# Gate and up weights of a macaron encoder block: split tiles of their own, 224 bytes off the 2 KB raster

## The chip, the cores and the metric

The kernel runs as one program on one core of a Trainium2 chip. The metric is the device time of one execution in microseconds (us), the median of several runs. SBUF, the memory that the engines work from, has 128 partitions; an address here is a byte offset within each partition. TensorE (PE in the profile) multiplies a stationary operand, which is loaded ahead of it (PEld), by a moving operand that streams through, and adds the result up in PSUM. VectorE (DVE), ScalarE (ACT), GpSimd (POOL) and the DMA queues (SP issues most of them) work beside it.

## The reference

One encoder layer over 512 frames of width 1024 in float32: a SwiGLU feed-forward at half weight, a token mixer, a second SwiGLU feed-forward at half weight, each with an RMS norm before and after.

```
def swiglu(h, w_gate, w_up, w_down):
    return (jax.nn.silu(h @ w_gate) * (h @ w_up)) @ w_down      # 1024 -> 4096 -> 1024

h = rms_norm(x, g_ffn1_pre)
x = x + 0.5 * rms_norm(swiglu(h, w_ffn1_gate, w_ffn1_up, w_ffn1_down), g_ffn1_post)
h = rms_norm(x, g_mix_pre)
proj = h @ w_in                                                 # 1024 -> 5632
... stick-breaking attention (8 heads x 64), retention (4 heads x 128), sigmoid merge gates
x = x + rms_norm(merged @ w_out, g_mix_post)
h = rms_norm(x, g_ffn2_pre)
x = x + 0.5 * rms_norm(swiglu(h, w_ffn2_gate, w_ffn2_up, w_ffn2_down), g_ffn2_post)
```

Both feed-forwards compute h @ w_gate and h @ w_up with 4096 columns each. These two products are what the change is about.

## The kernel before

**Split products.** Every float32 operand of TensorE is split in two parts of a reduced float32 format, hi and lo: ScalarE writes hi (a copy that rounds), VectorE writes lo = whole - hi. A product of two operands is then three matmuls: hi by hi, hi by lo, lo by hi. So each block of weights, 4 KB in each partition (1024 values), needs a tile `w_hi` and a tile `w_lo`, both split out of `w_raw` (where the DMA lands) or out of `w_sum` (a sum of two raw blocks).

**Gate and up (both feed-forwards).** Gate and up are taken together as 2 x 2 blocks and multiplied by a scheme of seven products in place of eight (Strassen's, in Winograd's form): the tokens are halved (256 each), the contraction is halved (512 each), and gate and up columns of a pair are two column blocks of 128. The loop runs over 16 pairs (`NG`); the first pair is taken by eight plain products. In each later pair PE runs the seven products in the order `PE_ORDER`; `product_of` (L804) calls `blocks` (L781), which issues 24 matmuls, one after another: for each of two column blocks f and four contraction blocks k the stationary operand is 128 columns of `w_hi` or `w_lo` (512 bytes in each partition), and 256 token columns of `a1`, `a21`, `a22` or the sums `s1` to `s4` stream past (1024 bytes). Lines 792, 794 and 795 are hi by hi, hi by lo, lo by hi; 777, 779 and 780 are the same three for the very first half block. Each matmul comes with its own load of the stationary operand. `PLACE` gives each of the seven products its own pair of tiles.

**Down.** The second product of the feed-forward uses seven products too, but the other way round: the stationary operand is 128 tokens of `l_hi` or `l_lo`, and 512 columns of `w_hi` or `w_lo` stream past (`down_unit`, lines 893 to 895). Its weights use the first four of the tile pairs in turn (`SLOTS`); `l_hi` and `l_lo` lie over the last three.

**Mixer.** Projections take one of the first four tile pairs as stationary operand and stream 512 columns of `h_hi` or `h_lo` (`product`, lines 725 to 727), or the other way round (`row_product`, 732 to 734). Between them stand the attention's own matmuls. Some of these (lines 1056 to 1066) have as stationary operand `tri`, a small constant tile that lies behind the other constants at the end of the arena, and stream 128 to 512 columns of `sp_hi`, `sp_lo`, `cum_hi` or `cum_lo`.

**Where tiles lie.** All tiles are placed by hand in one arena by `place`, which gives an offset. The arena starts 128 bytes past a multiple of 2048. `x_tok`, `h_hi`, `h_lo`, `w_raw`, then `w_hi0`, `w_lo0` (with `w_sum0` at the same place as `w_lo0`), `w_hi1` and so on follow one another, and each is a multiple of 4 KB, so each starts on the arena's own raster of 2048 bytes; `act_at` and `region` are asserted to lie on it (`LINE`). `tri` lies off it: its two halves start 864 and 1376 bytes past a raster point. So of every address that PE reads in the gate and up stage, stationary or moving, the offset from the raster is a multiple of 512.

**Order.** Each engine has its own instruction list, written by hand, and waits on semaphores. In the gate and up stage a weight tile is written again one pair later, when `unit_done` says that PE has finished the product that read it (`return_wait`, L1288, on ACT; `free`, L1811, on DVE). At the last pair `chunk_hi` (L1418) begins to write `l_hi` over the tiles of products 1, 2 and 6, one chunk for each finished product.

Of the kernel before, what the change touches and what calls it, by code (L numbers as in the profile page):

```python
# [7 lines left out]
ALU = mybir.AluOpType  # L8
ACT = mybir.ActivationFunctionType
F32 = mybir.dt.float32  # L10
F32R = mybir.dt.float32r

P = 128
T = 512
# [7 lines left out]
PAIRS = SBH * SBD // P  # L22
RMS_EPS, GN_EPS = 1e-6, 1e-5
ARENA = 212832
UNIT = KD * P
SLOTS = 4
# [11 lines left out]
PRODUCTS = 7  # L38
# [12 lines left out]
LEFT = 3  # L51

PLACE = {7: 0, 5: 1, 4: 2, 3: 3, 1: 4, 2: 5, 6: 6}

RAW11, RAW21, RAW12, RAW22 = range(4)
# [41 lines left out]
CONST_COLS = 514  # L97
CONST_BYTES = 2080
LINE = 2048

def constants():
# [108 lines left out]
def build(nc, x, gains, w_gate1, w_up1, w_down1, w_in, w_proj_sb, w_proj_ret, w_out,  # L211
          w_gate2, w_up2, w_down2, const, decay_t, rope_t, x_mid, out):
    with ExitStack() as ctx:
# [3 lines left out]
        top = [0]  # L217

        def place(name, shape, dt=F32, at=None):
            size = -(-int(np.prod(shape[1:])) * 4 // 32) * 32  # L220
            off = top[0] if at is None else at
            if at is None:
                top[0] += size
            assert off + size <= ARENA, (name, off + size)
            return nc.alloc_sbuf_tensor_at(name, shape, dt, offset=base + off), off + size

        small_at = ARENA - 5 * 32 - 8 * P - CONST_BYTES
# [15 lines left out]
        h_lo, _ = place("h_lo", [P, KD, T], F32R)  # L244
        w_raw, _ = place("w_raw", [P, SLOTS, UNIT])

        w_hi, w_lo, w_sum = [], [], []
        for i in range(PRODUCTS):
            if i == SLOTS:

                mix_at = top[0]
            w_hi.append(place(f"w_hi{i}", [P, UNIT], F32R)[0])
            w_sum.append(place(f"w_sum{i}", [P, UNIT], at=top[0])[0])
            w_lo.append(place(f"w_lo{i}", [P, UNIT], F32R)[0])
        act_at = top[0]
        assert act_at % LINE == 0

# [53 lines left out]
        b22_hi, e = place("b22_hi", [P, UNIT], F32R, at=e)  # L313
        a21_hi, e = place("a21_hi", [P, KH, HALF], F32R, at=act_at + quarter + 4096)
        b22_lo, e = place("b22_lo", [P, UNIT], F32R, at=act_at + quarter + 12288)
# [6 lines left out]
        decay, e = place("decay", [P, RH, T], at=mix_at)  # L322
        rope, e = place("rope", [P, 2, T], at=e)
        region = e
        assert region % LINE == 0

        en = region + 6 * D * 4

# [16 lines left out]
        qk_r, e3 = place("qk_r", [P, 2, T], at=e3)  # L345
        g_r, e3 = place("g_r", [P, T], at=e3)
        proj_t, e3 = place("proj_t", [P, T], at=e3)
        oe = (small_at - 4 * PAIRS * T * 4) // LINE * LINE
        assert e3 <= oe, (e3, oe)
        o_sb_hi, e4 = place("o_sb_hi", [P, PAIRS, T], F32R, at=oe)  # L350
        o_sb_lo, e4 = place("o_sb_lo", [P, PAIRS, T], F32R, at=e4)
# [18 lines left out]
        w_hi_done, w_lo_done, unit_done = sem("w_hi_done"), sem("w_lo_done"), sem("unit_done")  # L370
# [142 lines left out]
        def bank_two(first):  # L513
# [5 lines left out]
        T_ORDER = (7, 6, 4, 5)  # L519
        N_SUMS = 3 * (NG - 1)  # L520

        FIRST_AT = {RAW11: (w_hi[PLACE[1]], w_lo[PLACE[1]]), RAW21: (w_hi[PLACE[2]], w_lo[PLACE[2]]),
                    RAW12: (w_hi[PLACE[6]], w_lo[PLACE[6]]), RAW22: (b22_hi, b22_lo)}

        block = ctx.enter_context(nc.Block())

# [175 lines left out]
        def _(pe):  # L702
# [99 lines left out]
            def product_of(m, bank):  # L802
                stream = {1: A11, 2: A12, 3: (s4_hi, s4_lo), 4: A22, 5: (s1_hi, s1_lo), 6: (s2_hi, s2_lo),
                          7: (s3_hi, s3_lo)}[m]  # L804
                blocks(bank, (w_hi[PLACE[m]], w_lo[PLACE[m]]), *stream, m in (1, 2, 7), m in (2, 3, 4)
                       ).then_inc(unit_done, 1)

            def first_gate(fi, u0, half, d):
# [199 lines left out]
            for ev in events:  # L1008
                if ev[0] == "mm":
                    f, k = ev[1], ev[2]  # L1010
# [166 lines left out]
        def _(act_eng):  # L1177
# [98 lines left out]
            def weights_hi(fi, u0, p, m):  # L1276

                slot = PLACE[m]
                if m in (1, 2, 3):
                    raw = {1: RAW11, 2: RAW21, 3: RAW22}[m]  # L1280
                    act_eng.wait_ge(raw_full[raw], p * 16 + (raw_turn(u0) * 16 + 16))
                    return_wait(u0, p, m)
                    act_eng.activation(w_hi[slot][:, :], w_raw[:, raw, :], ACT.Copy).then_inc(w_hi_done, 1)  # L1283
                else:
                    sum_made(fi, p, m)
                    act_eng.activation(w_hi[slot][:, :], w_sum[slot][:, :], ACT.Copy).then_inc(w_hi_done, 1)  # L1286

            def return_wait(u0, p, m):  # L1288

# [123 lines left out]
            def chunk_hi(fi, ud, n):  # L1413
                ph, c = divmod(n, CHUNKS)
                m = DOWN_ORDER[ph]

                act_eng.wait_ge(unit_done, ud + 2 * (n - LEFT) + 2 if n >= LEFT else ud - PRODUCTS + n + 1)
                if m == 1:  # L1418
                    act_eng.wait_ge(a_done, NF * fi + 2 * CHUNKS * (c + 1))
                elif m in (7, 6, 5, 3):  # L1420
                    act_eng.wait_ge(f_sum, 16 * fi + CHUNKS * (7, 6, 5, 3).index(m) + c + 1)
                act_eng.activation(l_hi[n % LEFT][:, :, :], left_of(m, c), ACT.Copy).then_inc(l_hi_done, 1)
# [251 lines left out]
        def _(dve):  # L1674
# [115 lines left out]
            def weights_lo(fi, u0, p, m):  # L1790
                slot = PLACE[m]
                dve.wait_ge(w_hi_done, p * PRODUCTS + (u0 + SPLIT_ORDER.index(m) + 1))
                if m in (1, 2, 3):
                    whole_w = w_raw[:, {1: RAW11, 2: RAW21, 3: RAW22}[m], :]
                else:
                    if m in (6, 7):

                        dve.wait_ge(t_done, p * 4 + (fi * N_T - {6: 1, 7: 2}[m]))
                    whole_w = w_sum[slot][:, :]
                dve.tensor_tensor(w_lo[slot][:, :], whole_w, w_hi[slot][:, :].bitcast(F32), ALU.subtract  # L1800
                                  ).then_inc(w_lo_done, 1)

            def first_lo(u0, i):
# [542 lines left out]
```

## Time and profile before

| | |
|---|---|
| device time, median of 3 runs | 1382.3 us (1382.27 to 1382.37) |
| span of the profiled execution, first to last instruction | 1380.3 us |
| outside the span | 2.0 us, the difference of the two (the profiled execution's own device time is not given beside its span) |
| PE busy / PEld busy | 1365.8 us (99%) / 1226.0 us (89%) |
| DVE busy / ACT busy | 1031.3 us (75%) / 734.2 us (53%) |
| DMA queue of SP | 34.6% of the 16 engines' span |

How to read it. "Busy" is the part of the span in which an engine has at least one instruction under way. PE's instructions overlap: one matmul is counted from its start until its last result is out, and the next has started long before that. The mean ns of one matmul is therefore not what it costs in a row of many; that is the distance from start to start, called the pitch below. The span goes from the first to the last instruction.

### The profile page before, as it was taken

The numbers are of one execution on the slowest core, as the hardware profiler recorded it, in microseconds if no ns is written. First come the engines' busy times: TensorE is split into PE (matmuls) and PEld (weight loads), VectorE is DVE, ScalarE is ACT, GpSimd is POOL, SyncE is SP. The second block draws the span as 40 slices with busy tenths as digits, with TensorE's granted clock in tenths as the row PEclk, the third lists the DMA queues.
The fourth block names the chain that finished last, engine by engine and source line by source line (L and its number), as shares of the span: only waits on it lengthen the run. The fifth ranks groups of instructions, "written<-read, shape, count | busy, mean of one in ns | idle before, by whom it ended". The sixth has DMA issues, their size and how long they took to land.

```text
span 1380.3 us, 22732 instructions
## 1 busy us (share of the span) xinstructions
PE 1365.8 (99%) x8668; PEld 1226.0 (89%) x8668; DVE 1031.3 (75%) x1124; ACT 734.2 (53%) x1008; POOL 99.9 (7%) x156
## 2 busy tenths in 40 slices
PE   8999999999999999999999999999999999999998
PEld 7999999999888888777778888899999999988886
DVE  7987887787988964767664344689778778888896
ACT  6544544545675652666663333555455445458563
POOL 0000000000340000222210000000000000025100
PEclk9999999999999999999999999999999999999999
DMA  6323332336995555212113345233233233399844
GB/s 206 108 83 115 122 96 86 122 108 237 193 206 156 175 206 132 68 58 64 47 46 92 92 132 188 92 122 116 85 122 108 79 117 122 100 283 197 178 142 153
DMA packets 152935, 177.71 MB, mean 129 GB/s; under 512 B 5552, under 2 KB 116400, under 8 KB 152752
## 3 DMA queue, kind: packets, MB, share of 16 engines
q1 hardware_dynamic: 139536, 151.54, 34.6%
q0 software_dynamic: 13056, 25.17, 10.1%
q8 instruction: 35, 0.57, 0.2%
q10 hardware_dynamic: 288, 0.26, 0.1%
q14 instruction: 20, 0.16, 0.0%
HBM read 170.66 MB, written 6.29 MB: 128 GB/s over the span
## 4 chain that ended last, share of the span: by engine, by line
PE 93%; DVE 3%; ACT 1%; DMA 1%; issue 1%; POOL 0%; SPq 0%; DVEq 0%; ACTq 0%; POOLq 0%
PE ps L792 15%; PE ps L795 15%; PE ps L794 15%; PE ps L893 7%; PE ps L894 7%; PE ps L895 7%; PE ps L725 6%; PE ps L727 5%; PE ps L726 5%; PE ps L732 2%; PE ps L734 2%; PE ps L733 2%; PE ps L1085 1%; DMA w_raw<-w_ffn_up 1%; PE ps L1040 1%; PE ps L1047 1%
## 5 line engine op out<-in xcount | busy, mean ns | idle before, releaser
L792 PE MATMUL ps<-s_hi,w_hi 128*128 128x256 f32 x960 | 271.9, 283 | 0.5 <-DVE w_lo L1800 0.5
L795 PE MATMUL ps<-s_hi,w_lo 128*128 128x256 f32 x960 | 271.7, 283 | 0.0
L794 PE MATMUL ps<-s_lo,w_hi 128*128 128x256 f32 x960 | 271.7, 283 | 0.0
L792 PE MATMUL ps<-a_hi,w_hi 128*128 128x256 f32 x808 | 229.0, 283 | 1.1 <-DVE a_lo L1755 1.1
L794 PE MATMUL ps<-a_lo,w_hi 128*128 128x256 f32 x808 | 228.7, 283 | 0.0
L795 PE MATMUL ps<-a_hi,w_lo 128*128 128x256 f32 x808 | 228.6, 283 | 0.0
L1286 ACT ACTIVATE w_hi<-w_sum 128x1024 fp32r<-128x1024 f32 x120 | 123.9, 1056 | 174.7 <-DVE w_sum L1829 80.1
L792 PEld LDWEIGHTS ps<-s_hi,w_hi 128*128 128x128 f32 x960 | 184.3, 192 | 0.8 <-DVE w_lo L1800 0.7
L794 PEld LDWEIGHTS ps<-s_lo,w_hi 128*128 128x128 f32 x960 | 184.3, 192 | 0.0
L795 PEld LDWEIGHTS ps<-s_hi,w_lo 128*128 128x128 f32 x960 | 184.3, 192 | 0.0
L893 PE MATMUL ps<-w_hi,l_hi 128*128 128x512 f32 x448 | 174.7, 390 | 0.0
L895 PE MATMUL ps<-w_hi,l_lo 128*128 128x512 f32 x448 | 174.4, 389 | 0.0
L894 PE MATMUL ps<-w_lo,l_hi 128*128 128x512 f32 x448 | 174.3, 389 | 0.0
L792 PEld LDWEIGHTS ps<-a_hi,w_hi 128*128 128x128 f32 x808 | 155.1, 192 | 1.5 <-issue 1.5
L794 PEld LDWEIGHTS ps<-a_lo,w_hi 128*128 128x128 f32 x808 | 155.1, 192 | 0.0
L795 PEld LDWEIGHTS ps<-a_hi,w_lo 128*128 128x128 f32 x808 | 155.1, 192 | 0.0
L1800 DVE TENSOR_TENSOR w_lo<-w_sum,w_hi 128x1024 fp32r<-128x1024 f32 x120 | 141.7, 1221 | 1.5 <-ACT w_hi L1286 1.1
L1678 DVE TENSOR_TENSOR w_lo<-w_raw,w_hi 128x1024 fp32r<-128x1024 f32 (+1 forms) x66 | 72.0, 1095 | 93.7 <-ACT w_hi L1186 93.3
L1800 DVE TENSOR_TENSOR w_lo<-w_raw,w_hi 128x1024 fp32r<-128x1024 f32 x90 | 109.9, 1223 | 37.0 <-ACT w_hi L1283 36.9
L2284 POOL DMA_DIRECT2D d_sum<-w_ffn_down x48 | 58.7, 1470 | 914.3 <-DVE w_raw L2001 860.3
L725 PE MATMUL ps<-h_hi,w_hi 128*128 128x512 f32 x288 | 118.6, 412 | 0.4 <-DVE w_lo L1678 0.4
L727 PE MATMUL ps<-h_hi,w_lo 128*128 128x512 f32 x288 | 112.5, 390 | 0.0
(222 smaller groups left out, 2529.1 us busy)
## 6 DMA issues: line engine op xcount, KB each, us to landing
w_raw<-w_ffn_gate SPq DMA_DIRECT2D x64, 512.0 KB, 5.0
w_raw<-w_ffn_up SPq DMA_DIRECT2D x64, 512.0 KB, 4.6
d_sum<-w_ffn_down POOLq DMA_DIRECT2D x48, 512.0 KB, 12.2
w_raw<-w_in SPq DMA_DIRECT2D x44, 512.0 KB, 3.9
w_raw<-w_ffn_down SPq DMA_DIRECT2D x40, 512.0 KB, 4.4
d_sum<-w_ffn_down SPq DMA_DIRECT2D x16, 512.0 KB, 7.9
x_tok<-x SPq DMA_DIRECT2D x8, 512.0 KB, 6.0
d_m_raw<-w_ffn_down SPq DMA_DIRECT2D x8, 512.0 KB, 8.3
```

The costliest lines, as they stand in the source:

```text
L725: pe.matmul(ps[:, bank, out_cols], wh, src_hi, start=first, stop=False)
L726: pe.matmul(ps[:, bank, out_cols], wh, src_lo, start=False, stop=False)
L727: return pe.matmul(ps[:, bank, out_cols], wl, src_hi, start=False, stop=last)
L792: pe.matmul(o, wh, hi[:, k, :], start=first and f == 0 and k == 0, stop=False, skip_group_check=True)
L794: pe.matmul(o, wh, lo[:, k, :], start=False, stop=False, skip_group_check=True)
L795: mm = pe.matmul(o, wl, hi[:, k, :], start=False, stop=last and k == KH - 1, skip_group_check=True)
L893: pe.matmul(o, sh, wh[:, cols], start=first and g == 0, stop=False, skip_group_check=True)
L894: pe.matmul(o, sh, wl[:, cols], start=False, stop=False, skip_group_check=True)
L895: mm = pe.matmul(o, sl, wh[:, cols], start=False, stop=last and g == 1, skip_group_check=True)
L1286: act_eng.activation(w_hi[slot][:, :], w_sum[slot][:, :], ACT.Copy).then_inc(w_hi_done, 1)
L1678: dve.tensor_tensor(w_lo[slot][:, 0:cols], w_raw[:, slot, 0:cols], w_hi[slot][:, 0:cols].bitcast(F32), ALU.subtract).then_inc(w_lo_done, 1)
L1800: dve.tensor_tensor(w_lo[slot][:, :], whole_w, w_hi[slot][:, :].bitcast(F32), ALU.subtract).then_inc(w_lo_done, 1)
```

## The change

The tiles that the gate and up stage uses are new ones, `u_hi`, `u_lo` and `w_sum` of each product. They lie where `w_hi` and `w_lo` lie, but 224 bytes higher (`UP_OFF`), so that each starts 224 bytes past a raster point. The stages that use `w_hi` and `w_lo` keep the names. Since the seventh `u_lo` now ends 224 bytes further up, and the fourth one too, everything from the fifth tile pair upward (`w_hi4` to `w_hi6`, `mix_at`, `act_at` and all that is placed from them: `l_hi`, `act`, `a21`, `b22`, `s3`, the mixer's tiles) moves up by 512 bytes (`GAP`); two asserts and one rounding that asked for 2048 now ask for 512. `b22`, the weights of one of the eight blocks of the first pair, is not among the `u` tiles: it moves by 512, not by 224. One wait changes: since a chunk of `l_hi` and `l_lo` now lies over the tiles of two products, `chunk_hi` waits for one product more (at most the third). No instruction is added, taken away or moved on any engine; only addresses differ, and that one count.

```diff
@@ build: the tiles @@
-        w_hi, w_lo, w_sum = [], [], []
+        w_hi, w_lo, u_hi, u_lo, w_sum = [], [], [], [], []
+        raster = top[0]
+        mix_at = raster + 2 * SLOTS * UNIT * 4 + GAP
         for i in range(PRODUCTS):
-            if i == SLOTS:
-
-                mix_at = top[0]
-            w_hi.append(place(f"w_hi{i}", [P, UNIT], F32R)[0])
-            w_sum.append(place(f"w_sum{i}", [P, UNIT], at=top[0])[0])
-            w_lo.append(place(f"w_lo{i}", [P, UNIT], F32R)[0])
-        act_at = top[0]
-        assert act_at % LINE == 0
+            at = raster + 2 * i * UNIT * 4 + (GAP if i >= SLOTS else 0)
+            w_hi.append(place(f"w_hi{i}", [P, UNIT], F32R, at=at)[0])
+            w_lo.append(place(f"w_lo{i}", [P, UNIT], F32R, at=at + UNIT * 4)[0])
+            at = raster + 2 * i * UNIT * 4
+            u_hi.append(place(f"u_hi{i}", [P, UNIT], F32R, at=at + UP_OFF)[0])
+            at += UNIT * 4
+            w_sum.append(place(f"w_sum{i}", [P, UNIT], at=at + UP_OFF)[0])
+            u_lo.append(place(f"u_lo{i}", [P, UNIT], F32R, at=at + UP_OFF)[0])
+        act_at = raster + 2 * PRODUCTS * UNIT * 4 + GAP
...
-        assert region % LINE == 0
+        assert region % GAP == 0
...
-        oe = (small_at - 4 * PAIRS * T * 4) // LINE * LINE
+        oe = (small_at - 4 * PAIRS * T * 4) // GAP * GAP
@@ the tiles that the first pair, the seven products and their splits use @@
-        FIRST_AT = {RAW11: (w_hi[PLACE[1]], w_lo[PLACE[1]]), RAW21: (w_hi[PLACE[2]], w_lo[PLACE[2]]),
-                    RAW12: (w_hi[PLACE[6]], w_lo[PLACE[6]]), RAW22: (b22_hi, b22_lo)}
+        FIRST_AT = {RAW11: (u_hi[PLACE[1]], u_lo[PLACE[1]]), RAW21: (u_hi[PLACE[2]], u_lo[PLACE[2]]),
+                    RAW12: (u_hi[PLACE[6]], u_lo[PLACE[6]]), RAW22: (b22_hi, b22_lo)}
...
-                blocks(bank, (w_hi[PLACE[m]], w_lo[PLACE[m]]), *stream, m in (1, 2, 7), m in (2, 3, 4)
+                blocks(bank, (u_hi[PLACE[m]], u_lo[PLACE[m]]), *stream, m in (1, 2, 7), m in (2, 3, 4)
...
-                    act_eng.activation(w_hi[slot][:, :], w_sum[slot][:, :], ACT.Copy).then_inc(w_hi_done, 1)
+                    act_eng.activation(u_hi[slot][:, :], w_sum[slot][:, :], ACT.Copy).then_inc(w_hi_done, 1)
...
-                act_eng.wait_ge(unit_done, ud + 2 * (n - LEFT) + 2 if n >= LEFT else ud - PRODUCTS + n + 1)
+                act_eng.wait_ge(unit_done, ud + 2 * (n - LEFT) + 2 if n >= LEFT else ud - PRODUCTS + min(n + 2, LEFT))
...
-                dve.tensor_tensor(w_lo[slot][:, :], whole_w, w_hi[slot][:, :].bitcast(F32), ALU.subtract
+                dve.tensor_tensor(u_lo[slot][:, :], whole_w, u_hi[slot][:, :].bitcast(F32), ALU.subtract
```

## Rows read from the trace of the kernel before

**Rows 1.** The page: busy time of two engines; the chain that ended last, by engine.
```profile
PE 1365.8 (99%) x8668; PEld 1226.0 (89%) x8668; DVE 1031.3 (75%) x1124; ACT 734.2 (53%) x1008; POOL 99.9 (7%) x156
PE 93%; DVE 3%; ACT 1%; DMA 1%; issue 1%; POOL 0%; SPq 0%; DVEq 0%; ACTq 0%; POOLq 0%
```

**Rows 2.** Groups of PE: line, output<-inputs, columns, xcount | busy us, mean ns
```profile
L792 PE MATMUL ps<-s_hi,w_hi 128*128 128x256 f32 x960 | 271.9, 283 | 0.5 <-DVE w_lo L1800 0.5
L792 PE MATMUL ps<-a_hi,w_hi 128*128 128x256 f32 x808 | 229.0, 283 | 1.1 <-DVE a_lo L1755 1.1
L792 PE MATMUL ps<-a_hi,b_hi 128*128 128x256 f32 x32 | 9.1, 286 | 0.0
L777 PE MATMUL ps<-a_hi,w_hi 128*128 128x256 f32 x8 | 2.4, 296 | 0.6 <-DVE a_lo L1740 0.6
L893 PE MATMUL ps<-w_hi,l_hi 128*128 128x512 f32 x448 | 174.7, 390 | 0.0
```

**Rows 3.** Windows inside both gate and up stages: busy us (xinstructions), PEclk, DMA.
```profile
core 0: us, PE busy (x) PEld busy (x) DVE busy (x) ACT busy (x) POOL busy (x), PEclk, DMA share, GB/s
100.00:200.00 100.00, 100.00 (x836) 100.00 (x835) 79.14 (x80) 49.56 (x60) 0.00 (x0) 1.00 0.34 105
950.00:1050.00 100.00, 100.00 (x836) 100.00 (x835) 80.47 (x81) 49.74 (x61) 0.00 (x0) 1.00 0.35 106
```

**Rows 4.** Timeline of PE in the gate and up stage: start us, duration us.
```profile
200.04 0.28 PE L792 MATMUL ps<-s_hi,w_hi 128*128 128x256 f32 x1
...
203.88 0.28 PE L795 MATMUL ps<-a_hi,w_lo 128*128 128x256 f32 x1
```

**Rows 5.** Timeline of PE in a mixer projection of 512 columns, settled.
```profile
569.05 0.39 PE L725 MATMUL ps<-h_hi,w_hi 128*128 128x512 f32 x1
569.28 0.39 PE L726 MATMUL ps<-h_lo,w_hi 128*128 128x512 f32 x1
569.50 0.39 PE L727 MATMUL ps<-h_hi,w_lo 128*128 128x512 f32 x1
569.73 0.39 PE L725 MATMUL ps<-h_hi,w_hi 128*128 128x512 f32 x1
```

**Rows 6.** Groups of PE in the window 572.44:573.70, stationary operand `tri`.
```profile
L1066 PE MATMUL ps<-cum_lo,tri 128*128 128x256 f32 x2 | 0.6, 280 | 0.0
L1064 PE MATMUL ps<-cum_hi,tri 128*128 128x256 f32 x2 | 0.6, 279 | 0.0
```

**Rows 7.** Groups of PE in the window 581.45:583.10, `tri` with 512 columns.
```profile
L1059 PE MATMUL ps<-sp_lo,tri 128*128 128x512 f32 x2 | 0.8, 397 | 0.0
L1056 PE MATMUL ps<-sp_hi,tri 128*128 128x512 f32 x2 | 0.8, 396 | 0.0
```

**Rows 8.** Groups of PE in 21.97:22.80, just after a gap, tiles on the raster.
```profile
L794 PE MATMUL ps<-a_lo,w_hi 128*128 128x256 f32 x3 | 0.8, 281 | 0.0
L795 PE MATMUL ps<-a_hi,w_lo 128*128 128x256 f32 x2 | 0.6, 280 | 0.0
```

**Rows 9.** Groups of PE in 567.10:568.30, just after a gap, 512 columns, on the raster.
```profile
L726 PE MATMUL ps<-h_lo,w_hi 128*128 128x512 f32 x2 | 0.8, 395 | 0.0
```

**Rows 10.** Timeline of the weight loads (PEld): two that follow the transposes.
```profile
21.75 0.19 PEld L792 LDWEIGHTS ps<-a_hi,w_hi 128*128 128x128 f32 x1
21.86 0.19 PEld L794 LDWEIGHTS ps<-a_lo,w_hi 128*128 128x128 f32 x1
```

**Rows 11.** Timeline of ACT at the end of the first gate and up stage.
```profile
330.20 0.60 ACT L1326 ACTIVATE u_c<-ps 128x512 f32<-128x512 f32 x1 [1.45 <-PE ps L795]
330.70 1.05 ACT L1422 ACTIVATE l_hi<-act 128x1024 fp32r<-128x1024 f32 x1
333.08 0.60 ACT L1334 ACTIVATE m_c<-ps 128x512 f32<-128x512 f32 x1 [1.33 <-PE ps L795]
333.58 1.05 ACT L1442 ACTIVATE w_hi<-w_raw 128x1024 fp32r<-128x1024 f32 x1
334.53 1.05 ACT L1422 ACTIVATE l_hi<-act 128x1024 fp32r<-128x1024 f32 x1
```

More of the change, by code:

```diff
@@ L99 @@
 LINE = 2048
+GAP = 512
+UP_OFF = 224
 def constants():
@@ L1282, in weights_hi @@
                     return_wait(u0, p, m)
-                    act_eng.activation(w_hi[slot][:, :], w_raw[:, raw, :], ACT.Copy).then_inc(w_hi_done, 1)
+                    act_eng.activation(u_hi[slot][:, :], w_raw[:, raw, :], ACT.Copy).then_inc(w_hi_done, 1)
                 else:
                     sum_made(fi, p, m)
-                    act_eng.activation(w_hi[slot][:, :], w_sum[slot][:, :], ACT.Copy).then_inc(w_hi_done, 1)
+                    act_eng.activation(u_hi[slot][:, :], w_sum[slot][:, :], ACT.Copy).then_inc(w_hi_done, 1)
             def return_wait(u0, p, m):
```

## The prediction

> **What bounds the kernel now.** I read the page first. PE is busy for 99% of the span, and 93% of the chain that ended last is PE [rows 1]. The table of groups shows why that share says little about single instructions: the matmuls of one form have a mean of 283 ns [rows 2], and the 5304 of them (counted below) end to end would be 1501 us, more than the span. So the next view is one that shows the pace. The windows in the middle of both gate and up stages have 836 matmuls in 100 us and PE without a gap [rows 3]. The timeline gives the pitch, from start to start: from 200.04 to 203.88 us there are 32 steps, so 120.0 ns each [rows 4]. In the 512-column products three steps take 0.68 us, 227 ns each [rows 5]. In both places the granted clock is at its upper level of 2.4 GHz (PEclk 1.00) [rows 3].
>
> From these two pitches: 256 more columns cost 107 ns, 0.418 ns a column, which is one cycle of 2.4 GHz. What is left is 120 - 107 = 13 ns per matmul, the same at 256 and at 512 columns. That fixed part is where a change of addresses could act. Nothing else in this stage can give time: PE never waits there, and DVE, next to it, is busy for 79% and 80% of it [rows 3].
>
> How many matmuls are concerned: three lines with 960 and 808 each, 3 x 1768 = 5304; three lines with 32 on `b_hi` and `b_lo`, 96; three with 8, 24 [rows 2]. Together 5424, at 120 ns 651 us, 47% of the span. The 96 on `b22` keep an offset that is a multiple of 512, so 5424 - 96 = 5328 get the new one.
>
> **The change part by part.** Nothing is issued more or less often, so every term is a change of duration.
>
> *The 224 bytes, seen by PE.* In the stage as it is, every pair of addresses that PE reads at one time is apart by a multiple of 512, and the pitch is 120 for all of them. The trace has one tile off the raster that PE reads as stationary operand, `tri`. With 256 columns its matmuls last 279 and 280 ns against 283 [rows 6, 2]. Duration and pitch go together: 283 with 120, 390 with 227 [rows 2, 4, 5], so the pitch is the duration less 163. For `tri` that makes 116 to 117 ns. I take 117, a saving of 3 ns, since the rows of `tri` are the nearest there are: same number of columns, same format, stationary operand off the raster. They aren't the same case. `tri` is 352 bytes past a multiple of 512 and the new tiles 224, and its matmuls come at most four in a row with others between. 5328 x 3.0 ns = 16.0 us.
>
> The bounds of this term. Below: two loads of such weights stand 110 ns apart at 21.75 and 21.86 us [rows 10], where the load did not have to share its time with a settled stream; each matmul needs one load, so I take 110 as the floor. 10 ns x 5328 = 53 us saved. Above: the same `tri` with 512 columns lasts 396 to 397 ns against 390, 7 ns more [rows 2, 7]. If 256 columns paid that, it would be 7 x 5328 = 37 us lost. Between ends this far apart I stay with the row of equal width.
>
> *A doubt, from the raster itself.* Durations of 280 and 281 ns also occur with all tiles on the raster, right behind a gap, before the stream goes back to 283 [rows 8]; at 512 columns the same phase costs more, 395 against 390 [rows 2, 9]. So the cost of a load beside a stream depends on how the two meet, and after a gap they meet otherwise than settled. This bears the term out in sign, shorter at 256 columns and longer at 512 when not in step, but says too that the short rows of `tri` may be an unsettled phase and not an effect of its address.
>
> Here the Trainium skill speaks against the change. In "TensorE: Matmul & The Clock Gate", section "Step-by-step: what each phase is for", it says that TensorE has two independent read ports, one for the moving operand and one for the weights, and that loading the next weights takes no read bandwidth from the running matmul. By that rule no address could matter and the sum would be 0; the 7 ns of [rows 7] do not fit it well. The same page's section "Back-to-back issue gap" gives N/2.4 + 2.5 ns, an estimate of 109 ns here, by which the sum would be -58 us if all of the excess were a collision; the trace's 120 is 11 ns above it.
>
> *The 512 bytes.* `l_hi`, `s3`, `a21`, `b22`, `act`, the mixer's tiles and `w_hi4` to `w_hi6` move by 512. PE reads today at offsets of 0, 512, 1024 and 1536 past the raster (the column blocks of a weight tile), with one pitch for all; the means and the 836 in 100 us leave no room for one slow quarter [rows 2, 3]. I cost it at 0.
>
> *ACT and DVE on the new tiles.* Their seven splits and four sums a pair now start 224 bytes off. No row shows such an operation alone. A pair takes 7 x 24 x 0.12 = 20.16 us, of which DVE is idle for a fifth, about 4.1 us [rows 3]; with 11 operations on these tiles each could grow by 0.37 us before PE waits. At 117 ns a pair lasts 19.66 us and the cover is 3.6 us; at the floor of 110 it is 18.5 us and 2.5 us. So 0, between no change and that cover; DVE would become the bound only below some 95 ns. ACT has half of its time free.
>
> *The later wait of `chunk_hi`.* Chunk 0 now waits for the second product of the last pair, chunk 1 for the third. On ACT chunk 0 stands behind the copy `u_c`, which itself waits for the third product and starts at 330.20; chunk 1 stands behind `m_c` and a split that start at 333.08 and 333.58 [rows 11]. Both waits are met before they are reached: 0. Without that cover chunk 0 would be a product later, 24 x 0.12 = 2.9 us, with the down splits of ACT and then of DVE queued behind it, and PE's first down unit behind those.
>
> **Sum.** -16.0 us on the span of 1380.3, 1364.3; the median of the runs is 2.0 us above the span, so 1366.3 us, 1.2% less.
>
> **The rivals.**
>
> *A, the forecast:* 116 to 118 ns settled, 1366 (1361 to 1372). For it: [rows 6]. Against it: [rows 8].
>
> *B, no effect:* the 13 ns are a fixed price of changing weights, and the stream settles at 120 wherever the tile lies. For it: the excess is the same at 256 and 512 columns, and four column blocks at four offsets make no difference; the rows of `tri` are short. Against it: `tri` is shorter in each group at 256 and longer at 512, as after a gap. Time: 1382.
>
> *C, much of the 13 ns is a collision that an offset takes away:* the pitch goes to between 110 and 114, near the floor of the load. For it: the spacing in [rows 10], and that an excess of 13 ns is there at all. Against it: nothing at 256 columns in the trace is settled below 116. At 112 ns: 8 x 5328 = 43 us, 1340 (1329 to 1350).
>
> *D, slower:* off the raster a load that is spread over two 512-byte pieces collides for longer, as in [rows 7]. Place: every matmul of `blocks`. Price: 7 ns, 37 us, 1420; it decides from a settled pitch of 120.5 on, since 0.5 ns x 5328 is 2.8 us. Against it: the same tile gains at 256 columns.
>
> The skill's rule on two ports is B's mechanism; that no address tells in the settled stream agrees with it [rows 3], the rows of `tri` don't [rows 6, 7].
>
> **How the numbers follow.** A 0.42, B 0.22, C 0.20, D 0.16. The forecast is A's 1366.3. What this kernel's measurement tells from no change is 0.2%, 2.8 us. Faster is A and C, 0.62; same is B, 0.22; slower is D, 0.16. The range reaches from C's floor, 1329, over A and B to 1386, which takes in a small loss; what is left out is nearly all of D.
>
> **What the profile after would show.** A: the mean of L792, L794 and L795 on `u_hi` and `u_lo` is 280 where it was 283, a window of 100 us in the stage has 857 matmuls in place of 836, and 32 steps take 3.74 us. The group on `b_hi` stays at 283 when settled, L893 at 390, and the mixer as it is. PE goes on without a gap in the windows. C: means of 273 to 277, and over 877 in the window. B: 283 and 836. D: 287 or more. The 512 bytes are wrong at zero if L893 or L725 move by 1 ns or more. The cover of DVE is wrong if PE in the windows shows idle time released by `u_lo`. The wait of `chunk_hi` is wrong if the first `l_hi` comes later after `u_c` than now, or if PE waits at the start of down. The forecast as a whole is wrong if the settled pitch is outside 116 to 118.

## The result, and the profile after

The changed kernel takes 1366.32 us, the median of four runs (1366.27, 1366.30, 1366.35 and 1368.69). The kernel before takes 1382.28 us in the same session. The ratio is 0.9889, 95% interval 0.9875 to 0.9903: 1.1% faster, 16.0 us. In the sessions of the later runs the kernel before took 1382.14 to 1382.32 us, so that all times below can be laid side by side. The profiled execution has a span of 1364.3 us against 1380.3.

The page of the changed kernel: busy time of the engines, the chain that ended last by engine, then groups (line, engine, operation, output<-inputs, shape, count | busy us, mean ns | idle before and who ended it). The lines are five further down than in the kernel before: L792, L794, L795 are now L797, L799, L800.

```profile
PE 1349.2 (99%) x8668; PEld 1209.1 (89%) x8668; DVE 1029.3 (75%) x1124; ACT 734.3 (54%) x1008; POOL 99.9 (7%) x156
PE 91%; DVE 4%; ACT 2%; DMA 1%; issue 1%; POOL 0%; SPq 0%; DVEq 0%; ACTq 0%; POOLq 0%
L797 PE MATMUL ps<-s_hi,u_hi 128*128 128x256 f32 x960 | 268.0, 279 | 1.5 <-DVE u_lo L1805 0.8
L797 PE MATMUL ps<-a_hi,u_hi 128*128 128x256 f32 x808 | 225.7, 279 | 1.1 <-DVE a_lo L1760 1.1
L1291 ACT ACTIVATE u_hi<-w_sum 128x1024 fp32r<-128x1024 f32 x120 | 124.0, 1057 | 173.0 <-DVE w_sum L1834 80.3
L797 PEld LDWEIGHTS ps<-s_hi,u_hi 128*128 128x128 f32 x960 | 180.5, 188 | 2.1 <-ACT m_c L1325 1.1
L898 PE MATMUL ps<-w_hi,l_hi 128*128 128x512 f32 x448 | 174.9, 390 | 0.1
```

Against [rows 2] the matmuls of the split weights went from 283 to 279 ns, and their idle time from 0.5 to 1.5 us. The products of `down` (L898) stayed at 390 ns. PE is still busy for 99%, but its share of the chain that ended last fell from 93% to 91%, and that of DVE rose from 3% to 4% [rows 1]. Both small moves mean something, as will be seen.

Windows in the middle of both gate and up stages, to be laid beside [rows 3], with the columns given there:

```profile
100.00:200.00 100.00, 100.00 (x860) 100.00 (x859) 81.68 (x83) 51.63 (x64) 0.00 (x0) 1.00 0.35 108
950.00:1050.00 100.00, 100.00 (x859) 100.00 (x859) 81.67 (x83) 49.64 (x60) 0.00 (x0) 1.00 0.34 105
```

And two rows of the timeline of PE, 32 steps apart, as in [rows 4] (start us, duration us):

```profile
200.06 0.28 PE L800 MATMUL ps<-a_hi,u_lo 128*128 128x256 f32 x1
...
203.79 0.28 PE L799 MATMUL ps<-s_lo,u_hi 128*128 128x256 f32 x1
```

24 matmuls more in 100 us, and 3.73 us for 32 steps where it was 3.84. With the starts in nanoseconds the mean pitch is 116.67, that is 280 cycles of 2.4 GHz in place of 288. At 512 columns it is 226.7 ns, 544 cycles, in both kernels. So I shall write the pitch as columns plus a number of cycles: N + 32 on the raster for both widths, and N + 24 for the new tiles.

From the first to the last matmul of a gate and up stage the time fell from 328.33 to 319.56 us in the first feed-forward and from 328.07 to 320.39 in the second, 16.46 us together (first start to last start). All the rest of the program got longer by 0.47 us. So the gain is where it was looked for.

### The profile page after: what moved, and what is told of

Same layout as the page of the kernel before. It is cut to its first block, busy times and chain, and to the rows that moved or that the text cites. A ratio compares the mean times of both kernels' runs of the same rounds, so it can differ in the third digit from the quotient of the medians.

```text
span 1364.3 us, 22732 instructions
## 1 busy us (share of the span) xinstructions
PE 1349.2 (99%) x8668; PEld 1209.1 (89%) x8668; DVE 1029.3 (75%) x1124; ACT 734.3 (54%) x1008; POOL 99.9 (7%) x156
## 4 chain that ended last, share of the span: by engine, by line
PE 91%; DVE 4%; ACT 2%; DMA 1%; issue 1%; POOL 0%; SPq 0%; DVEq 0%; ACTq 0%; POOLq 0%
PE ps L797 14%; PE ps L800 14%; PE ps L799 14%; PE ps L898 8%; PE ps L899 7%; PE ps L900 7%; PE ps L730 6%; PE ps L732 5%; PE ps L731 5%; PE ps L737 2%; PE ps L738 2%; PE ps L739 2%; PE ps L1090 1%; DMA w_raw<-w_ffn_up 1%; PE ps L1045 1%
## 5 line engine op out<-in xcount | busy, mean ns | idle before, releaser
L797 PE MATMUL ps<-s_hi,u_hi 128*128 128x256 f32 x960 | 268.0, 279 | 1.5 <-DVE u_lo L1805 0.8
L800 PE MATMUL ps<-s_hi,u_lo 128*128 128x256 f32 x960 | 267.7, 279 | 0.0
L799 PE MATMUL ps<-s_lo,u_hi 128*128 128x256 f32 x960 | 267.7, 279 | 0.0
L797 PE MATMUL ps<-a_hi,u_hi 128*128 128x256 f32 x808 | 225.7, 279 | 1.1 <-DVE a_lo L1760 1.1
L800 PE MATMUL ps<-a_hi,u_lo 128*128 128x256 f32 x808 | 225.4, 279 | 0.0
L799 PE MATMUL ps<-a_lo,u_hi 128*128 128x256 f32 x808 | 225.3, 279 | 0.0
L1291 ACT ACTIVATE u_hi<-w_sum 128x1024 fp32r<-128x1024 f32 x120 | 124.0, 1057 | 173.0 <-DVE w_sum L1834 80.3
L797 PEld LDWEIGHTS ps<-s_hi,u_hi 128*128 128x128 f32 x960 | 180.5, 188 | 2.1 <-ACT m_c L1325 1.1
L799 PEld LDWEIGHTS ps<-s_lo,u_hi 128*128 128x128 f32 x960 | 180.5, 188 | 0.0
L800 PEld LDWEIGHTS ps<-s_hi,u_lo 128*128 128x128 f32 x960 | 180.5, 188 | 0.0
L898 PE MATMUL ps<-w_hi,l_hi 128*128 128x512 f32 x448 | 174.9, 390 | 0.1
L797 PEld LDWEIGHTS ps<-a_hi,u_hi 128*128 128x128 f32 x808 | 151.9, 188 | 1.6 <-issue 1.5
L799 PEld LDWEIGHTS ps<-a_lo,u_hi 128*128 128x128 f32 x808 | 151.9, 188 | 0.0
L800 PEld LDWEIGHTS ps<-a_hi,u_lo 128*128 128x128 f32 x808 | 151.9, 188 | 0.0
L1805 DVE TENSOR_TENSOR u_lo<-w_sum,u_hi 128x1024 fp32r<-128x1024 f32 x120 | 141.6, 1219 | 1.5 <-ACT u_hi L1291 1.1
```

The lines of the kernel that those rows point to most:

```text
L797: pe.matmul(o, wh, hi[:, k, :], start=first and f == 0 and k == 0, stop=False, skip_group_check=True)
L799: pe.matmul(o, wh, lo[:, k, :], start=False, stop=False, skip_group_check=True)
L800: mm = pe.matmul(o, wl, hi[:, k, :], start=False, stop=last and k == KH - 1, skip_group_check=True)
L898: pe.matmul(o, sh, wh[:, cols], start=first and g == 0, stop=False, skip_group_check=True)
L1291: act_eng.activation(u_hi[slot][:, :], w_sum[slot][:, :], ACT.Copy).then_inc(w_hi_done, 1)
L1805: dve.tensor_tensor(u_lo[slot][:, :], whole_w, u_hi[slot][:, :].bitcast(F32), ALU.subtract).then_inc(w_lo_done, 1)
```

## The experiments

Two things had to be told apart first: the change has two edits (224 bytes for the split tiles, 512 bytes for the others, with the wait of `chunk_hi`), and my theory was that only the first acts. Then came what the 224 bytes do. "Distance" below is the address of the stationary operand less that of the streamed one, modulo 512.

**gap_only: the 512 bytes and the wait alone.**

```
-UP_OFF = 224
+UP_OFF = 0
```

> All addresses of the change but the 224: the gate and up weights stand on the raster again (offset 0), everything from the fifth tile pair up stays 512 bytes higher, and the later wait of chunk_hi stays. Theory (the gain is the 224 bytes as PE's weight loads see them): settled pitch 120 ns (duration 283), 836 matmuls in 100 us, and 1382.3 us within 0.1%. Rival (part of the gain, or a hidden loss, comes from the 512 bytes or the wait): another time, 1366 to 1381 if the 512 bytes help, over 1384 if they cost.

Measured: 1382.27 us, the median of 11 runs (1382.05 to 1382.53), ratio to the kernel before 1.0000, interval 0.9991 to 1.0009. The windows of it:

```profile
100.00:200.00 100.00, 100.00 (x836) 100.00 (x835) 79.12 (x80) 49.55 (x60) 0.00 (x0) 1.00 0.34 105
950.00:1050.00 100.00, 100.00 (x836) 100.00 (x835) 80.18 (x81) 49.73 (x61) 0.00 (x0) 1.00 0.35 107
```

836 as before, and the time too. The whole gain belongs to the 224 bytes.

**all_off: the weights of the mixer and of `down` 224 bytes off as well.**

```
-w_hi.append(place(..., at=at)[0])
-w_lo.append(place(..., at=at + UNIT * 4)[0])
+w_hi.append(place(..., at=at + UP_OFF)[0])
+w_lo.append(place(..., at=at + UNIT * 4 + UP_OFF)[0])
```

> The tiles of the down stage and of the mixer get the 224 bytes too, so all weights of all stages stand off the raster. There, matmuls of 512 columns run: 1344 in down and 384 in the mixer with the weights as the moving operand, 1056 with the weights as the stationary one, settled at 227 ns. Theory (as the short rows of tri at 512 columns showed, 396 to 397 ns against 390): +7 ns each where the load or the stream is off the raster, 2784 x 7 = 19 us, so about 1386 us. Rival (a settled stream gains at 512 columns as it did at 256, 3.3 ns each): 2784 x 3.3 = 9 us less than the changed kernel, 1357 us. Second rival (only the stationary operand's address counts, and the moving one's does not): down as in the changed kernel, the mixer's 1056 alone move.

Measured: 1380.89 us, ratio to the kernel before 0.9993 (0.9984 to 1.0002). One of its 11 runs was at 1386.06, the others between 1380.71 and 1381.03. Gate and up kept their new pace, and the 512-column matmuls lost what it had brought. Timeline of PE in the mixer of this kernel, to be laid beside [rows 5]:

```profile
749.69 0.40 PE L730 MATMUL ps<-h_hi,w_hi 128*128 128x512 f32 x1
749.92 0.39 PE L731 MATMUL ps<-h_lo,w_hi 128*128 128x512 f32 x1
750.15 0.40 PE L732 MATMUL ps<-h_hi,w_lo 128*128 128x512 f32 x1
750.39 0.39 PE L730 MATMUL ps<-h_hi,w_hi 128*128 128x512 f32 x1
```

A window and one group of the same kernel:

```profile
100.00:200.00 100.00, 100.00 (x860) 100.00 (x859) 81.64 (x83) 51.59 (x64) 0.00 (x0) 1.00 0.35 108
```

```profile
L898 PE MATMUL ps<-w_hi,l_hi 128*128 128x512 f32 x448 | 177.4, 396 | 0.0
```

Three steps take 0.70 us where they took 0.68: the mean is 233.3 ns, N + 48. `down` moved by the same amount, 390 to 396 ns, although there the weights are the streamed operand and `l_hi` the stationary one. Added up over the 2746 steps of this width from one product with weights to the next, the stream takes 647.3 us where it took 631.9 in the changed kernel, so 15.4 more, and the kernel is 14.6 us longer. The expectation had 19 us, from 7 ns each; one reason may be that those of the mixer with stationary weights have a mean of 227.8 ns in the changed kernel, not 226.7, so they had less to lose. The price that [rows 7] shows for `tri` was real and holds in a settled stream; it belongs to 512 columns.

**scan_low and scan_high: other offsets, one for each of the seven tile places.**

```
-UP_OFF = 224
+UP_OFFS = (0, 32, 64, 96, 128, 160, 192)          # scan_low
+UP_OFFS = (224, 256, 288, 320, 352, 384, 448)     # scan_high
... at=at + UP_OFFS[i]
```

> The seven products have their weights at seven offsets: product 7 at 0, 5 at 32, 4 at 64, 3 at 96, 1 at 128, 2 at 160, 6 at 192 bytes past the raster. One profile then shows seven pitches. Theory 1 (fine grain: what counts is whether the offset is an odd multiple of 32 bytes, as 224 and the 352 of tri are): 117 ns at 32, 96 and 160, 120 at 0, 64, 128 and 192. Theory 2 (a load that lies over a 512-byte boundary is the cheap one): 120 at 0 alone, 117 at all others. Theory 3 (the offset in time between the load's reads and the stream's counts): graded, from 120 at 0 falling towards 117 near 224. The whole between 1366 and 1382 us.

> The same with product 7 at 224, 5 at 256, 4 at 288, 3 at 320, 1 at 352, 2 at 384, 6 at 448 bytes. Theory 1 (odd multiples of 32): 117 at 224, 288 and 352, 120 at 256, 320, 384 and 448. Theory 2 (512-byte boundary): 117 at all seven. Theory 3 (graded): 117 or less around 224 to 288, rising to 120 towards 448. The whole between 1366 and 1382 us, or under 1366 if an offset is better than 224.

One run each: 1374.47 and 1372.87 us. The mean pitch by offset, over both stages:

```
offset      0     32     64     96    128    160    192
ns      119.5  118.3  117.7  117.4  118.4  120.0  117.7
offset    224    256    288    320    352    384    448
ns      117.8  120.1  118.1  114.3  119.7  118.5  117.9   first feed-forward
        117.7  119.8  118.3  117.7  117.5  118.3  117.6   second feed-forward
```

None of the three theories stands. Odd multiples of 32 are not a class of their own (160 costs as much as 0), and a load that lies over a 512-byte boundary is not the cheap one (160 again, and 256). But 256 costs what 0 costs, 288 what 32 costs. And 320 gave two different means in one run. In the first feed-forward, 320 settled within three matmuls of each group; ten steps of it in scan_high:

```profile
96.01 0.28 PE L799 MATMUL ps<-s_lo,u_hi 128*128 128x256 f32 x1
...
97.14 0.28 PE L800 MATMUL ps<-s_hi,u_lo 128*128 128x256 f32 x1
```

That is 113 ns, a pitch that my forecast had only for its case C. Groups of 24 with neighbours of other offsets are a mixed state, so the next runs held one offset through a whole stage.

**shift_all_b: the kernel before, with all its tiles but the constants 96 bytes further on.**

```
-offset=base + off
+offset=base + off + (SHIFT if off < small_at else 0)      # SHIFT = 96
```

> The kernel before with all its tiles but the small constants group at the end moved together by 96 bytes: weights and streams keep their distance in multiples of 512, only their absolute address changes. Theory (the distance between the addresses that PE reads at one time counts): 120 ns and 227 ns as before, 1382.3 us. Rival (the absolute address of the weights counts, as if a load that does not start on its boundary were the cheap one): a pitch under 119 in the gate and up stage, 1364 to 1377 us; and at 512 columns 233 in place of 227, as in the kernel with all weights off the raster.

Measured: 1382.20 us, the median of 10 runs (1381.99 to 1382.57), ratio to the kernel before 1.0001 (0.9991 to 1.0011); 835 and 836 matmuls in the two windows. So an address off the raster does nothing by itself. What acts is where the tiles lie to each other.

**Three kernels with two offsets, one in each feed-forward.** Each stage has a set of split tiles of its own; the rest is as in the change.

```
-UP_OFF = 224
+UP_OFFS = (320, 96)     # or (64, 192), or (288, 448), indexed by the feed-forward
```

> The first feed-forward has its gate and up weights 320 bytes off the raster, the second 96 bytes, each for the whole stage, so that the stream can settle. In the kernels with seven offsets in one stage it did not (116.7 at 224 when alone, 117.8 among others), so their means don't tell which is best. Theory (each distance has its own settled pitch, and the order of the mixed means holds): 320 settles under 116.7, at 113 to 116, and 96 near 117. Rival (off the raster one settled price for all, 24 cycles a load): 116.7 in both stages.

> 64 bytes in the first feed-forward, 192 in the second. Theory (each distance its own price, mixed means 117.8 and 117.6): 116 to 119, not equal. Rival (one price off the raster): 116.7 in both. A third reading, that multiples of 64 count as on the raster, would give 120 in both; the mixed means speak against it.

> 288 bytes in the first feed-forward, 448 in the second. 288 and 224 lie equally far from 256, 448 and 64 equally far from the raster. Theory (each distance its own price, in a circle of 512 bytes but not symmetric, since a load reads ahead of a stream): 288 differs from the 116.7 of 224, 448 from what 64 gives. Rival (one price off the raster): 116.7 in both.

One run each: 1360.13, 1361.09 and 1372.53 us. Windows of the three kernels, in this order:

```profile
100.00:200.00 100.00, 100.00 (x885) 100.00 (x884) 84.45 (x85) 52.06 (x65) 0.00 (x0) 1.00 0.39 120
950.00:1050.00 100.00, 100.00 (x855) 100.00 (x854) 80.48 (x82) 50.95 (x62) 0.00 (x0) 1.00 0.35 107
```

```profile
100.00:200.00 100.00, 100.00 (x885) 100.00 (x884) 84.45 (x85) 52.05 (x65) 0.00 (x0) 1.00 0.39 120
950.00:1050.00 100.00, 100.00 (x852) 100.00 (x851) 80.38 (x81) 50.66 (x62) 0.00 (x0) 1.00 0.35 107
```

```profile
100.00:200.00 100.00, 100.00 (x848) 100.00 (x847) 80.24 (x82) 50.24 (x61) 0.00 (x0) 1.00 0.34 105
950.00:1050.00 100.00, 100.00 (x852) 100.00 (x851) 80.31 (x81) 49.95 (x61) 0.00 (x0) 1.00 0.34 105
```

The settled pitches are 113.3 ns for 320 and for 64 (N + 16), 117.3 for 96, 117.8 for 192 and for 448, 118.3 for 288. So each distance has a price of its own, and the rival (116.7 for all) is out. Offsets that differ by 256 agree (0 and 256, 32 and 288, 64 and 320, 192 and 448), so I read the price as one of the distance modulo 256. One thing in the second feed-forward doesn't fit one price for each distance: at 192 and at 448 the last products of the first pair and the first two of the next ran at 113.3 ns, and behind the wait ahead of product 6 the pitch was 117.8 for the rest of the stage. In [rows 6] `tri` lies at 352, which is 96 modulo 256, and 96 settles with durations of 280 ns: the short rows of `tri` were the effect of its address, and my doubt about an unsettled phase was not needed for them.

**u64: one offset of 64 for all seven places.**

```
-UP_OFF = 224
+UP_OFF = 64
```

> The changed kernel with 64 in place of 224, in both feed-forwards. Theory (the price of a load beside a settled stream depends on the distance between load and stream modulo 256 bytes: 32 cycles of 2.4 GHz at 0, 24 at 224, 16 at 64): pitch 113.3 ns, 880 matmuls or a few more in 100 us, and 5328 x 3.3 = 17.8 us under the changed kernel, less 1 us that PE waits more in the first pairs: 1349 to 1351 us. Rival (113.3 is near what DVE or the loads allow, and the second feed-forward does not reach it): 1352 to 1360 us, with PE waiting for u_lo in the windows.

Measured: 1360.98 us, ratio to the kernel before 0.9819 (0.9793 to 0.9844). The theory had 1349 to 1351, and the six runs lie on three levels: 1351.1 and 1351.3; 1360.9, 1361.0 and 1361.2; 1371.2. Five are faster than the change, one is slower. The profiled run was the slowest, and its windows are:

```profile
100.00:200.00 100.00, 100.00 (x851) 100.00 (x850) 80.74 (x83) 50.66 (x62) 0.00 (x0) 1.00 0.34 105
950.00:1050.00 100.00, 100.00 (x852) 100.00 (x851) 80.31 (x82) 50.20 (x61) 0.00 (x0) 1.00 0.34 105
```

Its pitch is 117.8 ns in both stages, where the same offset had 113.3 in two_64_192_b. So one offset has two paces, and each can hold through a stage. The first gate and up stage took 322.5 us here and 312.5 in two_64_192_b, 10.0 us apart, which is the distance between two levels. So I read the levels as none, one or both feed-forwards at the fast pace; the fast levels themselves were not profiled in this kernel.

**all_64: the other weights at 64 too** (the edit of all_off, with 64).

> The same 64 bytes for the weights of the down stage and the mixer too. In the mixer's 1056 matmuls with the weights as the stationary operand the distance is then 64, in the 1728 where the weights stream it is -64, that is 192 modulo 256. Theory (the same distance is cheap at 512 columns as at 256, as 224 is not: 16 cycles where the load is the later address): under 227 ns in the mixer's projections, 220 to 226; at 192 dearer than 227. Rival (at 512 columns the raster is the best there is, since the load needs only half of the stream's time and any other distance costs more): 228 to 234 in both.

One run: 1358.53 us. Windows and two groups:

```profile
100.00:200.00 100.00, 100.00 (x885) 100.00 (x884) 84.46 (x85) 52.16 (x65) 0.00 (x0) 1.00 0.38 120
950.00:1050.00 100.00, 100.00 (x885) 100.00 (x884) 84.46 (x86) 52.92 (x64) 0.00 (x0) 1.00 0.37 114
```

```profile
L898 PE MATMUL ps<-w_hi,l_hi 128*128 128x512 f32 x448 | 174.4, 389 | 0.0
L899 PE MATMUL ps<-w_lo,l_hi 128*128 128x512 f32 x448 | 175.7, 392 | 0.0
```

Both stages at the fast pace here. The 512-column matmuls pay 233.2 ns in the mixer, where the distance is 64, and a mean of 229.0 in `down`, where it is -64, that is 192 modulo 256. On the raster they pay 226.7. So the rival's 228 to 234 holds, and the theory's 220 to 226 doesn't. Less what this costs (the mixer and the two `down` stages are 8.1 us longer than in u64), the kernel would have taken 1350.5 us, near the fastest level of u64.

**l64: u64 with the activations of `down` (`l_hi`, `l_lo`) moved to 64 modulo 256,** to ask if a distance of +64 would help at 512 columns, in the stage where -64 cost little.

> u64, and in the down stage l_hi and l_lo, the stationary operand there, stand 64 bytes off the raster (at 320, which is 64 modulo 256), while the streaming weights stay on it: 1344 matmuls of 512 columns at distance 64. Theory: the distance of 64 costs 16 cycles at 512 columns too, 220 ns, 1344 x 6.7 = 9 us under u64. Rival (the raster is the best at 512 columns): 228 to 234 ns, 2 to 9 us over u64.

Measured: 1373.91 us (two runs near 1368.7, two near 1379.1), ratio to the kernel before 0.9927 (0.9901 to 0.9954). `down` settled at 233.3 ns and its group at

```profile
L899 PE MATMUL ps<-w_hi,l_hi 128*128 128x512 f32 x448 | 177.3, 396 | 0.0
```

So no: of the distances tried (0, 32, 64, 192, 224), the raster is the best for 512 columns. The two levels, 10.4 us apart, are the upper two of u64 again, some 8 us higher, which is about what 1340 matmuls cost at 6.6 ns more (8.8 us).

**reset64: can the fast pace be forced?** In the profiles with one offset to a stage the pace changed only at two kinds of place: where PE had waited, and where it passed a group on the raster (the product with `b22`, which no variant takes off the raster).

```
-UP_OFF = 224
+UP_OFFS = (64, 256, 288, 320, 320, 320, 320)
```

> Only the offsets of the gate and up tiles differ from the change: 64 for product 7, 256 for 5, 288 for 4, and 320 (64 modulo 256) for 3, 1, 2 and 6. Product 5 is in effect on the raster again, and is passed once in every pair. Theory (the phase in which a group of matmuls begins decides which of the two regimes an offset of 64 modulo 256 gets; the group on the raster wipes the phase that came before, and from 288 to 320 the stream falls to 113.3 ns, as product 3 did in each pair of the scan from 224 to 448): five products at 113.3 ns, product 5 at 120 and product 4 at 118.2, mean 115.0 ns, 5.0 ns less than the kernel before, 5328 x 5.0 = 26.6 us, some 1356 us, with all runs within 0.2% of each other. Rival 1 (the draw takes place at the gaps of PE alone, and passing an offset changes nothing): levels some 10 us apart between runs, as with one offset of 64 for all, and a regime that stays the same through a stage. Rival 2 (behind 0 and 32 the stream goes to the slow regime of 117.5, as product 4 did in the scan from 0 to 192): 7 products at a mean of 118 ns, some 1372 us, all runs alike.

One sentence in that expectation is wrong: product 3 reached 113.3 in the settled pairs of the first feed-forward of scan_high only, not in the second (118). Measured: 1372.79 us, the median of 5 runs (1372.07 to 1373.10), ratio to the kernel before 0.9931 (0.9917 to 0.9944). That is rival 2, 1372 with all runs alike, and my theory fell. The profile shows how. Timeline of PE at the end of product 7 (offset 64), in product 5 (offset 256), and further on at offset 320:

```profile
941.52 0.28 PE L797 MATMUL ps<-s_hi,u_hi 128*128 128x256 f32 x1
...
945.26 0.28 PE L797 MATMUL ps<-s_hi,u_hi 128*128 128x256 f32 x1
...
945.62 0.28 PE L797 MATMUL ps<-s_hi,u_hi 128*128 128x256 f32 x1
...
948.02 0.28 PE L800 MATMUL ps<-s_hi,u_lo 128*128 128x256 f32 x1
...
955.10 0.28 PE L800 MATMUL ps<-a_hi,u_lo 128*128 128x256 f32 x1
...
959.81 0.28 PE L797 MATMUL ps<-s_hi,u_hi 128*128 128x256 f32 x1
```

33 steps of 113.3 ns, behind a wait. Then 20 steps of 120.0 on what is in effect the raster. Then 40 steps of 117.8 at an offset that had 113.3 in two_320_96_b, and this pace at that offset for the rest of the stage. The levels are gone because the fast pace has no chance to last.

Does a group on the raster always lead to the slow pace? The traces say no, and show what goes with it. Behind the groups with `b22` in the first pair of a stage, 64 and 320 came out at 117.8 ns in 15 of 16 passes of the kernels that held them for a whole stage. The sixteenth is in the second feed-forward of all_64 (two starts behind the first group with `b_hi`, 69 steps apart, then two behind the second, 40 apart):

```profile
897.07 0.28 PE L797 MATMUL ps<-a_hi,u_hi 128*128 128x256 f32 x1
...
904.89 0.28 PE L797 MATMUL ps<-a_hi,u_hi 128*128 128x256 f32 x1
...
908.35 0.28 PE L800 MATMUL ps<-a_hi,u_lo 128*128 128x256 f32 x1
...
913.06 0.28 PE L797 MATMUL ps<-a_hi,u_hi 128*128 128x256 f32 x1
```

113.3 ns first, 117.8 then. Both groups have a mean of 120.0 ns when the first steps are left out. But in nanoseconds the second one goes 120, 120, 120, and the first one 118, 117, 121, 120, 124, over and over. scan_high has the same pair of patterns at its offset of 256: the same five unequal steps (within 1 ns) in all 15 pairs of the first feed-forward, where 320, two products further on, falls to 113.3, and 120s, even within 1 ns or so, in all 15 of the second, where 320 stays at 117.8. In reset64 the steps are even in all 30 passes, and only once did 320 run at 113.3 behind them, with a short wait of PE in between (at 930.63 us). So the raster doesn't wipe the history: the stream has two rhythms there as well, with one mean, and in these traces the even one led to the slow pace at 64 and 320, the uneven one to the fast. At 192 and 448 the pitch behind even 120s was 113.3, in four of four passes. So 117.8 may be one of two settled paces of 192 and 448 too; no run held the fast one for a stage.

## Why the prediction was right

The forecast was 1366.3 us, of case A, and the measurement 1366.32. The mechanism was right: the 224 bytes shorten the pitch, and the other edits cost nothing. That the two numbers agree to 0.1 us is luck: two terms were off, against each other, and the main one was read from a tile at another distance.

*The count and the pace.* The 5328 matmuls are right. The term of 3.0 ns was taken from durations in whole nanoseconds and is 3.33 in the trace (120.0 to 116.67), so the term is 17.8 us and not 16.0. The mean of the group is 279 where I said 280, the window has 860 where I said 857, and 32 steps take 3.73 us where I said 3.74. The `b_hi` group keeps 283 ns as its median, as its distance, still a multiple of 512, asks. The prediction cites [rows 3] for the clock in the mixer too, which those windows don't cover; a window of 568 to 570 us shows PEclk 1.00 there as well.

*The row that the term was read from.* The rows of `tri` did show an effect of address, but not that of 224 bytes: its distance counts as 96, and 96 has a pace of 117.3 when settled. That 224 has nearly the same, 116.7, nobody could read from `tri`. Had `tri` lain at 64, the same reading would have given 113 or 118.

*The 512 bytes and the wait of `chunk_hi`.* Both together at zero in gap_only, 1382.27 against 1382.28 us. In the changed kernel's timeline of ACT the first `l_hi` still starts 0.50 us behind the start of `u_c`, as in [rows 11]:

```profile
321.82 0.60 ACT L1331 ACTIVATE u_c<-ps 128x512 f32<-128x512 f32 x1 [1.23 <-PE ps L800]
322.32 1.05 ACT L1427 ACTIVATE l_hi<-act 128x1024 fp32r<-128x1024 f32 x1
```

*The cover of ACT and DVE.* The splits cost the same off the raster (ACT 1057 ns where it was 1056, DVE 1219 where it was 1221), so the address term is zero. But "a faster PE meets no wait" was read off the settled windows, and pairs 1 and 2 of the second feed-forward are not settled. PE's rows with a wait there, in the changed kernel:

```profile
915.88 0.38 PE L797 MATMUL ps<-s_hi,u_hi 128*128 128x256 f32 x1 [0.85 <-DVE u_lo L1805]
...
936.40 0.39 PE L797 MATMUL ps<-s_hi,u_hi 128*128 128x256 f32 x1 [0.65 <-ACT m_c L1325]
```

Before, the first of these was 0.45 us (the 0.5 in [rows 2]), and in place of the second was a start only 0.14 us late, without idle time. The chain of waits, followed back from there in the changed kernel (start us, length us), shows whose pace it is; the first eight rows lead to the first wait, the others, later, to the second:

```profile
904.41 0.68 DVE act L1884
905.09 2.27 DVE s_lo L1792 x2
907.36 0.82 DVE u_lo L1805
908.42 1.22 DVE u_lo L1805
909.63 1.15 DVE w_sum L1829
910.80 1.24 DVE w_sum L1841
912.22 1.05 issue
913.27 1.23 DVE w_sum L1848
...
923.35 3.87 DMA w_raw<-w_ffn_up
...
934.83 1.04 ACT u_hi L1291
935.87 0.49 ACT m_c L1325
```

The chain has no piece of PE between 899.84 and 936.40 us. Ahead of the first wait DVE has the streamed sums and the weights to do at once. From its `act` to PE's start this takes 11.47 us (904.41 to 915.88), and it took 11.47 before (913.01 to 924.48): PE only comes earlier to the same queue. The second wait ends behind DVE, one DMA of the up weights and two operations of ACT, where in the kernel before the chain of this stretch was PE's own. Over both stages the starts of product 6 were late by 0.75 us before (the step less the pitch) and by 2.00 in the changed kernel. This 1.2 us, with the 0.5 of the other stages, takes 17.8 down to the 16.0 that was measured. My prediction named this sign ("if PE in the windows shows idle time released by `u_lo`"), but looked for it in windows that leave those pairs out.

*The rivals.* B (no effect) is out at this offset. D is out at 256 columns and true at 512, as all_off shows: +6.6 ns a matmul, near the 7 that I took. C is not what 224 bytes do, but its mechanism exists: at 64 a settled pace of 113.3 is there, and a run of u64 took 1351.1 us. That C's lower bound of 110 would ever be reached is not borne out; nothing went below 113.

*The rule on two read ports.* The Trainium skill, "TensorE: Matmul & The Clock Gate", "Step-by-step: what each phase is for", says that loading weights takes no read bandwidth from the running matmul. These runs don't bear out that the two leave each other alone: with the same loads and matmuls the pitch is 113.3, 116.7, 117.3, 117.8, 118.3 or 120.0 ns by the distance of the two addresses, and shifting both leaves it as it was. The estimate of 109 ns from the section "Back-to-back issue gap" of the same page was not reached at any of the distances; the page gives that formula for a single matmul by itself.

## What stays open

The runs show that the pitch depends on the distance of the two operands and on the way in which the stream was entered. They don't show what collides. That it is these two reads, and not PE's against those of DVE, ACT or the DMA, is argued: shift_all_b left all those distances alone too, but the pitch is the same in every settled pair while DVE and ACT start and stop. That distances count modulo 256 rests on four pairs of offsets, most of them with one profile for each. Offsets between the multiples of 32 were not tried. Which wait leads to which pace is not settled: 64 came out of its waits now fast, now slow. The run of the changed kernel at 1368.69 and that of all_off at 1386.06 have no profile, so it is not shown that 224 has one pace alone.

## What to carry to other kernels

When PE is busy without a gap, look at the pitch and not at the share or the duration: 120 ns for 256 columns of a 4-byte format, with new weights for each matmul, holds 13 ns that are not columns, and up to half of them depend on the layout. Set the distance between stationary and streamed tiles for each stage apart, by its number of columns, since the offset that gains 3 ns at 256 costs 7 at 512. And take several runs before trusting an offset: 64 is 0.4% better than 224 in the median, but its runs spread over 20 us, and three of the four at 224 agree within 0.1.

## What was not expected of the hardware

- The two paces at 64 each hold for 260 us and more, and which of them comes makes a stage 10 us longer or shorter (312.5 and 322.5 us); runs of one program lay at 1351, 1361 and 1371 us (u64). A single run, or a single profile, of such a kernel says little.
- On the raster one mean of 120.0 ns hides two rhythms, even steps and five unequal ones (118, 117, 121, 120, 124), and the pace that followed at 64 or 320 bytes went with the rhythm in every pass but one, where PE had waited in between. A mean can't tell them apart, single starts in nanoseconds can.
- The duration in the records moves with the pitch, 283 to 279 ns for 120.0 to 116.7 and the loads 192 to 188, so a few nanoseconds in a mean of many matmuls are a real change of pace.
